# Modulation pieces, sliding means and decay products moved in a two-block fp32 kernel on one core

## What is computed

```
mod = silu(c) @ w_ada + b_ada          # 1024 -> 6144, one row; the same for block 2
h   = rmsnorm(x) * (1 + scale_m) + shift_m
z, xbc, dt, u_pool, gates = split(h @ w_in)
y   = ssd_chunked_scan(xs*dt, dt*a, b, c)     # 4 groups, 4 chunks of 128 tokens,
                                              # exp(segsum) decay matrices per head
y_pool = causal_multiscale_pool(u_pool)       # mean over the last 2, 4, 8 or 16 tokens
                                              # (fewer at the start), minus u_pool,
                                              # 256 channels for each window
x  += gate_m * ((g_ssd*y_ssd + g_pool*y_pool) @ w_out)
x  += gate_f * (relu(h2 @ w_up)**2 @ w_down)  # h2: normed and modulated with shift_f, scale_f
```

## Time and profile before

| | |
|---|---|
| time of 3 runs | 1857.09 us median (1852.63 to 1859.3) |
| profiled execution: its time / its span | 1854.17 us / 1852.4 us |
| mean granted PE clock | 0.949 of full speed |
| busy: PE / DVE / ACT / POOL | 91% / 48% / 34% / 43% of the span |
| moved by DMA | 194.32 MB, 105 GB/s on average |

### The profile page before, as it was taken

How to read it: one execution, slowest core, us unless ns; L and a number is a source line. 1 busy time by engine, 2 the same in 40 slices (tenths; PEclk the granted TensorE clock), 3 DMA queues, 4 the chain that set the end, 5 groups by cost and what they waited for, 6 DMA issues and landing times.

```text
span 1852.4 us, 20603 instructions
## 1 busy us (share of the span) xinstructions
PE 1681.6 (91%) x7578; PEld 1351.5 (73%) x7578; DVE 884.6 (48%) x1165; ACT 634.1 (34%) x824; POOL 796.4 (43%) x636
## 2 busy tenths in 40 slices
PE   3988999999899999799999997989857799999995
PEld 2666778787688877588888886768746477888784
DVE  5536454555645352643344455564744755113324
ACT  3434434343223222432133222444123444334421
POOL 1263545555344544345545552313243255444441
PEclk7889999999899999899999997979979899999998
DMA  8111112122135534145544441211011033222221
GB/s 315 46 68 44 71 69 91 69 69 91 68 113 183 182 136 159 68 147 180 189 149 143 170 182 55 85 46 60 33 46 68 23 136 108 94 105 91 85 94 60
DMA packets 35234, 194.32 MB, mean 105 GB/s; under 512 B 3904, under 2 KB 4160, under 8 KB 19776
## 3 DMA queue, kind: packets, MB, share of 16 engines
q1 hardware_dynamic: 23616, 151.06, 22.7%
q10 hardware_dynamic: 11520, 41.95, 6.5%
HBM read 190.90 MB, written 2.10 MB: 104 GB/s over the span
## 4 chain that ended last, share of the span: by engine, by line
PE 72%; DVE 14%; POOL 5%; ACT 4%; issue 3%; DMA 2%; DVEq 0%; SPq 0%; ACTq 0%; POOLq 0%
PE main L727 56%; PE main L723 8%; POOL w_lo L573 5%; ACT w_hi L1027 2%; DVE rstd L1624 1%; PE auxB L751 1%; DMA raw<-stream 1%; DVE h_lo L1654 1%; PE auxD L830 1%; DMA ada_first<-w_ada 1%; DVE tmp L1419 1%; PE auxD L895 1%; DVE tmp L1562 1%; DVE x L1639 1%; DVE ysum L1638 1%
## 5 line engine op out<-in xcount | busy, mean ns | idle before, releaser
L573 POOL TENSOR_TENSOR w_lo<-raw,w_hi 128x512 fp32r<-128x512 f32 (+1 forms) x522 | 703.5, 1379 | 854.8 <-ACT w_hi L1027 854.5
L727 PE MATMUL main<-h_hi,w_hi 128*128 128x512 f32 (+2 forms) x1136 | 458.5, 404 | 38.5 <-DVE h_lo L1654 16.4
L727 PE MATMUL main<-h_lo,w_hi 128*128 128x512 f32 (+2 forms) x1136 | 449.8, 396 | 0.0
L727 PE MATMUL main<-h_hi,w_lo 128*128 128x512 f32 (+2 forms) x1136 | 449.5, 396 | 0.0
L1027 ACT ACTIVATE w_hi<-raw 128x2048 fp32r<-128x2048 f32 (+3 forms) x136 | 247.9, 1823 | 269.9 <-PE main L727 230.5
L727 PEld LDWEIGHTS main<-h_hi,w_hi 128*128 128x128 f32 (+2 forms) x1136 | 216.0, 190 | 106.6 <-issue 25.7
L727 PEld LDWEIGHTS main<-h_hi,w_lo 128*128 128x128 f32 (+2 forms) x1136 | 216.1, 190 | 48.8 <-issue 1.0
L727 PEld LDWEIGHTS main<-h_lo,w_hi 128*128 128x128 f32 (+2 forms) x1136 | 216.6, 191 | 44.1 <-issue 0.5
L1562 DVE SCALAR_TENSOR_TENSOR tmp<-main,par,tmp 128x511 f32<-128x511 f32 x88 | 65.9, 749 | 176.3 <-ACT tmp L1128 174.7
L1587 DVE SCALAR_TENSOR_TENSOR ada_acc<-ada_raw,cs,ada_acc 128x1024 f32<-128x1024 f32 x70 | 114.3, 1634 | 29.4 <-DMA ada_raw<-w_ada 20.8
L723 PE MATMUL main<-w_hi,h_hi 128*128 128x512 f32 (+1 forms) x256 | 101.7, 397 | 19.8 <-POOL w_lo L573 10.2
(11 more groups left out here) (351 smaller groups left out, 2381.0 us busy)
## 6 DMA issues: line engine op xcount, KB each, us to landing
raw<-stream SPq DMA_DIRECT2D x118, 1024.0 KB, 4.9
ada_raw<-w_ada ACTq DMA_DIRECT2D x80, 512.0 KB, 4.4
ada_first<-w_ada SPq DMA_DIRECT2D x16, 512.0 KB, 6.5
raw<-stream SPq DMA_DIRECT2D x8, 768.0 KB, 4.2
raw<-stream SPq DMA_DIRECT2D x8, 640.0 KB, 3.8
x<-x_in SPq DMA_DIRECT2D x2, 2048.0 KB, 9.4
out<-x SPq DMA_DIRECT2D x8, 256.0 KB, 2.0
con<-consts SPq DMA_DIRECT2D x1, 486.0 KB, 3.6
```

The costliest lines, as they stand in the source:

```text
L573: ins = nc.gpsimd.tensor_tensor(w_lo[:, s, a:b], raw[:, s, a:b], w_hi[:, s, a:b], ALU.subtract)
L727: ins = nc.tensor.matmul(bank[0:n, :], w[:, k, col:col + n], a[:, ka_, :], start=start, stop=stop)
```

## The change

It does four things. `ada_slots` puts 24 modulation pieces over GS, PW, GP, BP and OUT0 to OUT1, one or two in each, where before two stood in each unit from GS0 to BP2. `ada_sum` moves from the end of the eighth piece's unit to the middle of the next, save where the next unit needs it. The windows move two half units later, the small copies give way to one scan of the first w columns, and `p_lo` of a window is made at the next window step instead of at once. POOL's four decay products move from the end of X1 to the middle of BC, that is behind the `w_lo` of Z0 instead of ahead of it.

```diff
@@ ada_slots @@
-    slots = [n for n in range(gs0, gs0 + 12) for s in both]
+    slots = [n for n in range(gs0, gs0 + 4) for s in both] + [gs0 + 4]
+    slots += [n for n in range(gs0 + 5, gs0 + 8) for s in both] + [gs0 + 8]
+    slots += [n for n in range(gs0 + 9, gs0 + 13)] + [n for n in range(gs0 + 13, gs0 + 15) for s in both]
@@ plan_steps @@
+    mid[find("BC")] += [("seg_fill", 0)]
...
     for n, t in enumerate(WINDOW_ORDER):
-        slot(2 * at["U"][0] + 1 + n).append(("window", t))
+        slot(2 * at["U"][0] + 3 + n).append(("window", t))
+    slot(2 * at["U"][0] + 3 + KD).append(("window_last", 0))
...
+    ada_due = (at["UP"][0], at["KV"][0], at["FU"][0])
     for p, n in enumerate(ada_slots(at)):
         mid[n].append(("ada_piece", p))
         if p + 2 < 80:
             end[n].append(("ada_load", p + 2))
         if p % 8 == 7:
-            end[n].append(("ada_sum", p // 8 + 2))
+            (end[n] if n + 1 in ada_due else mid[n + 1]).append(("ada_sum", p // 8 + 2))
@@ DVE, window @@
-                if n:
-                    dve.wait_ge(pl_lo, n)
+                if n:
+                    window_lo(n - 1)
                 u = xs_tok[:, t // 4, t % 4, :]
-                src, d, slot = u, 1, 0
+                src, d, slot, whole = u, 1, 0, 0
                 while d < w:
                     dst = tmp[:, 2 + slot, :]
-                    nc.vector.tensor_copy(dst[:, 0:d], src[:, 0:d])
-                    link(tt(dst[:, d:SEQ], src[:, d:SEQ], src[:, 0:SEQ - d], ALU.add))
+                    whole += d
+                    link(tt(dst[:, whole:SEQ], src[:, whole:SEQ], src[:, whole - d:SEQ - d], ALU.add))
                     src, d, slot = dst, 2 * d, 1 - slot
+                link(nc.vector.tensor_tensor_scan(src[:, 0:w], u[:, 0:w], nothing[:, 0:w], 0.0, ALU.add, ALU.add))
...
                 dve.sem_inc(win_ready, 1)
+
+            def window_lo(n):
+                t = WINDOW_ORDER[n]
                 dve.wait_ge(pl_hi, n + 1)
-                tt(p_lo[:, t, :], src, p_hi[:, t, :], ALU.subtract).then_inc(pl_lo, 1)
+                link(tt(p_lo[:, t, :], tmp[:, win_slot(t), :], p_hi[:, t, :], ALU.subtract))
+                dve.sem_inc(pl_lo, 1)
```

## The result

The changed kernel takes 1846.43 us (median of 5 runs, 1845.97 to 1847.99); the kernel before took 1857.09 us beside it (5 runs, 1852.63 to 1859.3). The ratio is 0.9944, with a 95% interval of 0.9929 to 0.996: 10.4 us faster (7.4 to 13.2). The profiled execution took 1846.05 us, its span is 1844.1.

The account below looks back on a forecast made before the run. PE, busy 91% of the span, bounds the kernel; only its waits and slow clock can shrink. -5.2 - 6.4 - 1.7 - 0.3 = -13.6 against 1854.17 gives 1840.6, taken as 1842.0 between two bases; range 1835 to 1851.

Parts of the forecast that it names:

- the windows: Third U unit to GS0: moving the windows later cuts PE's waits and slow clock from 13.9 to 7.5 us, -6.4 us.
- the pieces: Modulation pieces and sums: 7.6 us go at GS3, BP0 and BP2, 5.9 come at OUT2, net -1.7 us.
- the fill: Z0 of group 0: POOL's decay products behind the first `w_lo` let PE start earlier, -5.2 us.
- the rival with 0.17: U units to Y1: DVE's chain keeps the gain, windows give -2.1, total -9.3, 1846 us; chance 0.17.
- -8.9: Total if OUT2 takes all that BP2 gave: modulation +3.0, time given as 1846 us; chance 0.14.
- -4.6: Total if DVE's chain keeps the windows' gain and OUT2 takes BP2's, together; time given as 1850 us.
- the fill's gain doesn't arrive: Z1 waits instead of Z0 if POOL's fill stretches over 1.1 us; costs at most 5.2, 1847 us; chance 0.05.
- Waste in all: Third and fourth U units before the change: PE's waits 2.98 and 5.66, slow clock 1.8 and 3.4, 13.9 us.
- The loss at OUT2: OUT2's weights come late behind x, two pieces and a queued load: wait 4.0, slow clock 1.9, +5.9 us (2.5 to 10.6).
- gone: 1.1 + 0.5 + 3.43 + 2.6 = 7.6 us: Waits before `ada_sum` at GS3 (1.1) and BP2 (0.5), PE's wait at BP2 (3.43) and slow clock (2.6) vanish.

Follow-up runs that it names:

- the cheaper windows: The kernel after, each full-length add of a window replaced by a multiplication by 2, running sums left out; 1844.09 us in one execution.
- the fill alone: The kernel before with only POOL's decay products moved behind the weight split of Z0; 1851.65 us, ratio 0.9966.
- mixed windows: The kernel after with windows mostly at unit middles, two at the ends of the third U unit and Y0; 1845.94 us, ratio 0.9939.

## Why the prediction was right, and where it wasn't

The forecast was 1842.0 with a range of 1835 to 1851; measured are 1846.4. The gain was put at 13.6 us against the profiled execution and is about 10.4 in the medians. That the kernel gets faster by over 0.3% and where most of PE's waits go was right. Of the three large terms one was right, and two were wrong in opposite directions: the windows gave 6.4 us less than forecast, the pieces 2.9 more (the fill 1.1 more). That the sum still came within 4.4 us is in part luck. For the windows the mechanism that happened is that of the rival with 0.17, whose time was 1846; it still gave them 2.1 us.

Two of the rivals' times are rounded down in the prediction: with its own base of 1855.6, -8.9 makes 1846.7 and -4.6 makes 1851.0. No conclusion hangs on it.

**Decay products: predicted -5.2 (bounds -5.8 to -2.9), measured -6.3 (-8.5 to -4.1) by the times, -5.5 by the traces.** From BC's end to the middle of the first U unit four traces without the part take 365.8 to 368.3 us, mean 367.0; ten with it 360.9 to 362.6, mean 361.5. The step was right in each piece: `w_lo` took 4.96 (I had 5.56 for it), PE waited 3.3 us, Z1 showed no wait. The slow clock behind the wait mostly stayed: 24 matmuls took 7.1 to 8.5 us in the four traces without the part and 7.3 to 8.5 in eight of the ten with it.

In the other two (after with the old windows, and the cheaper windows) they took 5.7, at a granted clock of 1.00. There Z1 does wait, 1.0 us in both:

```profile
115.45 0.50 PE L727 MATMUL main<-w_hi,h_hi 128*128 128x512 f32 x1 [0.99 <-POOL w_lo L577]
```

That is the wait of the rival "the fill's gain doesn't arrive", by way of a faster PE and not of a stretched fill, and the gain arrived all the same: 360.9 and 361.5 us from BC's end.

**Windows: predicted -6.4 (bounds -9.2 to -2.1), measured nothing.** Alone it is +1.7, with an interval of -0.2 to +3.5, so that even the small end of the bounds was too large. On top of the rest it is +0.7 by the ratios and -0.2 by the medians, known to some 3.6 us only.

*The waste was counted rightly.* "Waste in all: 2.98 + 1.8 + 5.66 + 3.4 = 13.9 us": the kernel with one window per unit, which has no wait there, takes 62.0 us from the middle of the first U unit to GS0, the kernel before 75.8, which is 13.7 more (with the changed kernel's 73.8 it is 11.8, where my sum left 7.5). But the 1.8 of slow clock in it has no price of its own. The fourth U unit's `w_lo` was set by DVE's third window, so PE's block between the two waits had no say in when the second ended. The kernel after with the old windows shows it: behind the same first wait its block ran at full clock, 11.2 us instead of 12.8, and the second wait was 7.3 instead of 5.66.

```profile
480.27 0.50 PE L731 MATMUL main<-h_hi,w_hi 128*128 128x512 f32 x1 [2.99 <-POOL w_lo L577]
498.75 0.80 PE L731 MATMUL main<-h_hi,w_hi 128*128 128x512 f32 x1 [7.30 <-POOL w_lo L577]
```

From one wait's end to the other's it is 18.48 us there and 18.47 before. What counts is when the fourth U unit starts, and that was forecast well: 7.2 us earlier against the mark (32.3 behind it instead of 39.5), where 2.98 + 1.8 + 5.66 - 3 makes 7.4.

*What failed is the step behind it: DVE's chain was put too fast.* I allowed "one more microsecond or three where `w_lo` runs beside it" and waits of 0.5 at Y0, 2 at Y1 and 0.2 at GS0. The second window took 7.3 us where a clean one of its kind took 3.4, and each `p_hi` and `p_lo` pair sits on the same chain. So the `w_hi` of the fourth U unit, Y0, Y1 and GS0 came 15.0, 13.2 and 13.6 us apart (482.95, 497.98, 511.16, 524.77), against 11.2 to 11.5 that a unit needs: PE falls into a wait in every unit. They were 3.4, 2.6, 1.1 and 2.2, 9.2 in all for my 5.7, with 2.6 of slower blocks for my 1.8. Of the 7.2 us that PE was ahead at the fourth U unit, 5.7 were left at Y0, 4.3 at Y1 and 1.9 at GS0. This is the second rival, "DVE's chain keeps what the windows gave", which had 0.17. Between the middle of the first U unit and GS0 the part did save 1.1 to 2.1 us in the traces. In the two kernels with the old pieces it didn't last: the wait ahead of BP2's sum was 1.8 and 3.3 us there, against 0.5 and 1.4 with the old places. In the changed kernel 1.1 us remain in the trace, which the times don't resolve.

**Pieces: predicted -1.7 (bounds -5.1 to +3.0), measured -4.6 (-6.5 to -2.8).** The loss at OUT2 was sized well: 5.9 predicted, 3.6 of wait and 1.9 of slow clock measured (3.1 and 3.1 with the pieces alone), by the mechanism named, load 23 and `w_hi` behind pieces 20 and 21. OUT3 had no wait. OUT0 has one of 1.2 us in all kernels with the new pieces but two, in which PE waits at BP3 instead; I hadn't seen it coming. Too small was what goes: "gone: 1.1 + 0.5 + 3.43 + 2.6 = 7.6 us" has no slow clock behind the two sums, because the one execution that I read had 0 and 0.4 there. Three others had 1.5 to 2.8 and 1.8 to 2.4, some 4 us together. That these, less the 1.2 at OUT0, are the 3 us between forecast and measurement is argued from four traces of the old pieces against the ones of the new, not shown by a run of its own.

**The base.** The same execution was a light one, 1854.17 where the median of 35 runs is 1858.32. I saw the 2.9 us to the median of three and put the base between; the slow blocks just named are of that size.

**What would show it.** Right: the 3.3 us at Z0, no wait at the third U unit and BP2, about 3 at the fourth, one of 3.6 at OUT2, behind ACT's queued loads. Wrong: "small ones at Y0 and Y1", which are 2.6 and 1.1; 0.2 at GS0, which has 2.2; and the wait at OUT0, a stage that the prediction didn't name.

## What to carry to other kernels

- Before a slow block behind a wait is priced, ask what sets the next wait. Where both hang on one chain of another engine, PE's block between them is slack: when it ran 1.6 us faster, the second wait was 1.6 us longer. What a moved chain gives is read at the last unit that hangs on it: 7.2 us ahead at the first such unit were 1.9 three units later.
- Work that must be done before a fixed point moves its wait along when it is moved. What helped was to find units whose engine was idle (the first two U units), with one piece in each BP unit behind them; that gave 6 us, where four rearrangements among busy units gave nothing.
- One profiled execution prices short waits badly. The slow blocks behind the same wait differ by up to 2.8 us between traces, which is the size of the terms in question here.

## What the runs showed of the hardware

- The price of one and the same wait isn't fixed. Behind a wait of 2.99 us at the third U unit, 48 matmuls took 12.84 us in the kernel with the fill alone (granted clock 0.87) and 11.18 in the kernel after with the old windows (1.00). In the windows view (columns as in the earlier trace rows), fill alone:

```profile
480.00:492.90 12.90, 12.84 (x48) 10.07 (x48) 9.91 (x24) 4.66 (x6) 0.77 (x1) 0.87 0.25 83
```

  and after with the old windows:

```profile
480.20:491.50 11.30, 11.17 (x48) 8.93 (x48) 8.37 (x22) 3.38 (x5) 0.02 (x1) 1.00 0.26 94
```

- At OUT2 a wait of 2.97 us (mixed windows) had 24 matmuls in 5.73 us behind it, waits of 3.1 to 4.0 in other kernels 7.2 to 8.6.
- The slow block at Z0 doesn't grow with the wait: 24 matmuls took 7.1 to 8.5 us behind a wait of 9.0 (four traces) and 5.7 to 8.5 behind one of 3.3 (ten traces).
- Short waits ahead of the sums' 16 one-column matmuls (0.5 to 3.3 us) were followed by slow blocks of up to 2.8 us, and in one trace, behind 1.1 us, by none.
- Beside a running `w_lo` DVE's instructions, copies too, are held about 1 us each: 16 columns took 1.2 us instead of 0.17, a scan of 8 columns 1.1 instead of 0.17, an add of 509 columns 1.7 instead of 0.7. In the four contended windows read above, of three different makes, exactly four were held, as many as `w_lo` has pieces. The number of DVE's instructions made no difference to that. No run has a `w_lo` of another number of pieces.
